# Attention weights of a two-layer trunk: turned by transfers and VectorE instead of TensorE, weighted sums one turn later

## The chip, the core and the metric

The kernel runs on one core of a Trainium2 chip. The metric is the device time of one execution in microseconds (us). Before the change it is 2096.89 us, the median of 3 runs (2096.42 to 2096.99). The engines are TensorE (PE in the profile; PEld is its weight load), VectorE (DVE), ScalarE (ACT), GpSimd (POOL) and SyncE (SP). SP and ACT issue DMA transfers, each into a queue of its own.

## The reference, cut to what matters

Two decoder layers over 256 tokens of width 2048 in float32. Layer 0 is a gated recurrence with an MLP, layer 1 is attention with an MLP. With a block of 256 keys and 256 tokens there are no past blocks, so the attention is plain causal attention with 16 heads of 128:

```python
qkv = (x @ w_qkv).reshape(bsz, seqlen, 3, ATTN_HEADS, ATTN_HEAD_DIM)
q = (_partial_rope(q, cos, sin) * (ATTN_HEAD_DIM ** -0.5)).transpose(0, 2, 1, 3)
k = _partial_rope(k, cos, sin).transpose(0, 2, 1, 3)
...
s_own = jnp.where(k_pos[None, :] <= q_pos[:, None], s_own, NEG_INF)
...
p = jax.nn.softmax(s, axis=-1).astype(v.dtype)
...
        + jnp.einsum("bhcp,bhpd->bhcd", p_own, v_own))
...
return o @ w_out
x = _layer_norm(DEEPNORM_ALPHA * x + y, ln_g[layer, 0], ln_b[layer, 0])
x = _layer_norm(DEEPNORM_ALPHA * x + _sqrelu_mlp(x, mlp_w1[layer], mlp_w2[layer]), ...)
```

## The kernel before, in words

**Turns and blocks.** Every product with a weight matrix is cut into turns. A turn makes 512 output columns out of all 2048 inputs; its weights come in 8 blocks of 256 x 512 numbers (512 KB each). A block is loaded by SP into one of four staging slots `wst`, rounded by ACT into `wh` (line 757), and what the rounding left out is put into `wl` by DVE (line 1014). `wh` and `wl` have eight slots. TensorE multiplies high by high, low by high and high by low part (`turn`, lines 396 to 420; `token_turn` and `token_step`, lines 422 to 440), and the sums stand in PSUM: `banks(0)` and `banks(1)` are its two halves of four banks, and successive turns alternate between them.

**Who waits for whom.** `off` counts blocks from the first of a turn; 0 to 7 are the turn's own and 8 onward are the next turn's. SP may load block X when `wl` of block X-4 is made (line 247). ACT splits a block when it has landed and TensorE is done with block `off` - 7 (lines 754 to 756); DVE follows. During a turn ACT and DVE therefore make the blocks of the next one: `splits(b, START, LATE)` are `off` 9 to 13, then comes the work at the end of the turn, then `splits(b, LATE, NEXT)`, `off` 14 to 16. Each engine works through its list in the written order.

**Attention.** Four groups g of four heads, three turns each: queries, keys, values (lines 693 to 743 on TensorE, 975 to 1003 on ACT, 1405 to 1456 on DVE). In the middle of the values turn TensorE computes the scores of the group (lines 713 and 714). DVE adds the mask and takes the maxima, ACT takes the exponentials (line 989), DVE multiplies by the inverse sums (lines 1445 and 1447) and gives `p_ready`. After the values turn ACT copies the values out of PSUM (line 994, `v_stored`). TensorE turns the weights `prob`, three 128 x 128 pieces a head (line 732); ACT copies each head back out of PSUM (line 997); TensorE makes the weighted sums of the values with them (lines 739 and 741), in float32, into banks 2 and 3 of the half. ACT and DVE split the result into `hid` (lines 1000 and 1453), the input of the output projection, and the next group's queries turn follows. The keys turn of a group waits for that `hid` (line 705), since it uses the same PSUM half.

**Output projection** (`out_unit`, lines 644, 924 and 1302): four turns. Blocks 0 to 5 of a turn use the heads of groups 0 to 2, blocks 6 and 7 those of group 3. `prepare` (line 1181) scales the residual for it. On ACT it begins with a square root (line 926), whose table has to be loaded.

**A pattern that exists already.** In the MLP the squared activations are turned by transfers and VectorE: SP writes four pieces to a buffer in memory and reads it back (lines 312 to 320), DVE transposes 32 x 32 squares (line 1320). There, too, the first two turns of the second product are interleaved (`W2_ORDER`, line 83: blocks 0 to 5 of turn 0, 0 to 5 of turn 1, 6 and 7 of turn 0, 6 and 7 of turn 1; lines 654 to 665).

Of the kernel before, what the change touches and what calls it, by code (L numbers as in the profile page):

```python
# [81 lines left out]
HELD = BLOCKS - KCH  # L82
W2_ORDER = [(t, kb) for lo, hi in ((0, HELD), (HELD, BLOCKS)) for t in range(2) for kb in range(lo, hi)]
# [6 lines left out]
def build_trunk(nc, x, ln_g, ln_b, mlp_w1, mlp_w2, rg_w_in, rg_conv_w, rg_conv_b, rg_gate_a_w,  # L90
                rg_gate_a_b, rg_gate_x_w, rg_gate_x_b, rg_lambda, rg_w_out, moba_w_qkv, moba_w_out,
                rope, out):
    with ExitStack() as ctx:
# [3 lines left out]
        def sem(name):  # L97
            return ctx.enter_context(nc.semaphore(name))
# [39 lines left out]
        prob = f2[:, 0:1536].rearrange("p (h n) -> p h n", n=3 * P)  # L138
        probt = f2[:, 1536:3072].rearrange("p (h n) -> p h n", n=3 * P)
# [70 lines left out]
        pt_done = sem("pt_done")  # L210
        pt_copied = sem("pt_copied")
# [13 lines left out]
        to_quad = by_quad.rearrange("(q t) (i n) -> i t q n", q=GROUP, i=GROUP)  # L225

# [15 lines left out]
        def _(sp):  # L242
# [109 lines left out]
            with sp.Fori(0, NG) as g:  # L352
                for part in range(3):
                    load_turn(moba_w_qkv[0], part * D + g * COLS,
                              B_QKV + (3 * g + part) * BLOCKS)
# [36 lines left out]
        def _(pe):  # L392
# [250 lines left out]

            def out_unit(b, ready, free, n):
                token_pair(hid, b, ready, free)
                last_pair(b + 2 * BLOCKS, ready, free + 2, n)

            def mlp(b0, ready_x, ready_h, free, n):
# [5 lines left out]
                def w2_pair(s):  # L654
                    b = b0 + NG * BLOCKS + s * SLAB_BLOCKS
                    for n, (t, kb) in enumerate(W2_ORDER):
                        if kb == 0:
                            pe.wait_ge(psum_free, free + NG + s * (2 * NG) + t - 1)
                        pe.wait_ge(pair_ready, ready_h + s * (2 * NG) + (kb + 1))
                        pe.wait_ge(wl_done, b + n + 1)  # L660
                        for c in range(kb * KCH, (kb + 1) * KCH):
                            for part, low in ((0, 0), (1, 0), (0, 1)):
                                for a in range(HALVES):
                                    mm = token_step(hid, t, a, c, part, low, n)
                        mm.then_inc(mm_done, 1)
# [27 lines left out]
            for it in range(NG // 2):  # L693
                for j in range(2):
                    g = it * 2 + j
                    X, Y = banks(j), banks(1 - j)
                    b = B_QKV + it * (6 * BLOCKS) + j * (3 * BLOCKS)


                    if g == 0:  # L700
                        begun_turn(1, b, R_LN1)
                    else:
                        turn(xin, j, b, R_LN1)

                    pe.wait_ge(pair_ready, it * 4 + (2 * j + R_ATT))
                    turn(xin, 1 - j, b + BLOCKS, R_LN1)

                    pe.wait_ge(qk_ready, it * 4 + 2 * j + 1)
                    for kb in range(BLOCKS):
                        if kb == BLOCKS // 2:  # L710
                            pe.wait_ge(qk_ready, it * 4 + 2 * j + 2)
                            for h in range(GROUP):
                                pe.matmul(Y[:, h, 0:P], qg[:, h, 0:P], kg[:, h, 0:P], start=True, stop=True)
                                mm = pe.matmul(Y[:, h, P:3 * P], qg[:, h, P:T], kg[:, h, :],  # L714
                                               start=True, stop=True)
                            mm.then_inc(scores_done, 1)
# [773 lines left out]
```

## Time and profile before

| | |
|---|---|
| median of 3 runs | 2096.89 us |
| profiled execution: its own time | 2096.86 us |
| profiled execution: span from the first to the last instruction | 2095.0 us |
| busy: PE, PEld | 100%, 84% |
| busy: DVE, ACT, POOL | 62%, 47%, 1% |
| attention turns in the span (about) | 1005 to 1298 us |
| granted TensorE clock | 1.000 |

The span is what the trace shows; 1.9 us of the execution's own time lie around it. A timeline line has the start of its first instruction, the time from there to the end of the last, and how many instructions were merged (x). Matmuls overlap: one of 512 columns shows 0.39 us, and the next starts 0.23 us after it. A float32 matmul appears as two instructions.

### The profile page before, as it was taken

The page shows a single profiled execution, that of the slowest core. Times are in us where ns is not written, and L with a number is a line of the kernel's source. Part 1 is how long each engine was busy: PE and PEld are TensorE (multiplying, and loading weights), DVE is VectorE, ACT ScalarE, POOL GpSimd, SP SyncE. Part 2 cuts the span into 40 slices and gives each one's busy share as a digit, 9 for nine tenths or more (in the row PEclk, how much of TensorE's full clock was granted, in tenths as well). Part 3 has the DMA queues.
Part 4 walks back from the last instruction along what each step waited for, and adds up shares of the span by engine and source line. Part 5 has one row for each costly group of instructions (what it writes and reads, how often), then busy time and mean ns, then how long its engine had stood idle before and what let it go on. Part 6 is the DMA issues. An engine that isn't in the chain of part 4 may idle for free.

```text
span 2095.0 us, 28820 instructions
## 1 busy us (share of the span) xinstructions
PE 2085.9 (100%) x9918; PEld 1749.5 (84%) x9918; DVE 1290.4 (62%) x1246; ACT 975.1 (47%) x1172; POOL 21.3 (1%) x16
## 2 busy tenths in 40 slices
PE   9999999999999999999999999999999999999999
PEld 8898888888888888888988888888888888888887
DVE  6869666665555565555766667675665554555565
ACT  5596455434444443443644445454434443443442
POOL 0000010000000000000000000010000000000000
PEclk9999999999999999999999999999999999999999
DMA  7665758766766766775654556658666766766763
GB/s 257 195 197 189 235 180 261 250 200 203 236 222 183 238 230 201 219 233 171 193 186 158 168 167 225 202 189 267 216 210 212 241 206 195 243 218 228 241 212 120
DMA packets 233547, 439.80 MB, mean 210 GB/s; under 512 B 15056, under 2 KB 37840, under 8 KB 232432
## 3 DMA queue, kind: packets, MB, share of 16 engines
q1 hardware_dynamic: 232032, 432.79, 65.2%
q10 hardware_dynamic: 1424, 5.77, 0.7%
q8 instruction: 60, 0.98, 0.2%
q14 instruction: 31, 0.25, 0.0%
HBM read 419.63 MB, written 18.87 MB: 209 GB/s over the span
## 4 chain that ended last, share of the span: by engine, by line
PE 99%; DMA 0%; ACT 0%; issue 0%; DVE 0%; ACTq 0%
PE ps L427 75%; PE ps L419 11%; PE ps L416 5%; PE ps L726 1%; PE ps L725 1%; PE ps L724 1%; PE ps L558 1%; PE ps L739 0%; DMA wst<-in_rg_w_in_dram 0%; PE ps L524 0%; PE ps L523 0%; PE ps L525 0%; PE ps L596 0%; PE ps L714 0%; PE ps L599 0%; PE ps L575 0%
## 5 line engine op out<-in xcount | busy, mean ns | idle before, releaser
L1014 DVE TENSOR_TENSOR wl<-wst,wh 128x1024 fp32r<-128x1024 f32 x743 | 887.8, 1219 | 327.3 <-ACT wh L757 324.0
L757 ACT ACTIVATE wh<-wst 128x1024 fp32r<-128x1024 f32 x743 | 769.8, 1059 | 649.1 <-PE ps L427 411.8
L427 PE MATMUL ps<-wh,hid 128*128 128x512 f32 x2560 | 695.9, 390 | 0.0
L427 PEld LDWEIGHTS ps<-wh,hid 128*128 128x128 f32 x2560 | 479.5, 188 | 98.9
L427 PE MATMUL ps<-wh,xin 128*128 128x512 f32 x2048 | 548.9, 389 | 0.0
L427 PEld LDWEIGHTS ps<-wh,xin 128*128 128x128 f32 x2048 | 383.9, 188 | 79.4
L427 PE MATMUL ps<-wl,hid 128*128 128x512 f32 x1280 | 404.6, 389 | 0.0
L419 PE MATMUL ps<-xin,wh 128*128 128x512 f32 x960 | 331.2, 395 | 0.8 <-DVE wl L1014 0.8
L427 PE MATMUL ps<-wl,xin 128*128 128x512 f32 x1024 | 315.2, 389 | 0.0
L427 PEld LDWEIGHTS ps<-wl,hid 128*128 128x128 f32 x1280 | 240.2, 188 | 50.0
L416 PE MATMUL ps<-xin,wl 128*128 128x256 f32 x960 | 256.8, 278 | 0.0
L427 PEld LDWEIGHTS ps<-wl,xin 128*128 128x128 f32 x1024 | 192.2, 188 | 39.9
L419 PEld LDWEIGHTS ps<-xin,wh 128*128 128x128 f32 x960 | 175.9, 188 | 37.8 <-issue 1.3
L416 PEld LDWEIGHTS ps<-xin,wl 128*128 128x128 f32 x960 | 180.4, 188 | 5.3
L1320 DVE STREAM_TRANSPOSE f<-f 128x1024 f32<-128x1024 f32 x32 | 39.9, 1245 | 180.9 <-DMA f<-sq_by_quad 180.9
L934 ACT ACTIVATE hid<-f 128x1024 fp32r<-128x1024 f32 x32 | 34.0, 1063 | 207.4 <-DVE f L1320 207.4
L1204 DVE TENSOR_TENSOR f<-f,ps 128x1024 f32<-128x1024 f32 x36 | 43.9, 1220 | 94.5 <-PE ps L427 94.5
L1344 DVE TENSOR_TENSOR f<-f 128x1024 f32<-128x1024 f32 x32 | 39.2, 1225 | 76.6 <-ACT f L949 76.6
L949 ACT ACTIVATE f<-ps 128x512 f32<-128x512 f32 x64 | 34.7, 595 | 81.0 <-PE ps L427 81.0
L724 PE MATMUL ps<-wh,xin 128*128 128x512 f32 x128 | 50.6, 395 | 0.0
L726 PE MATMUL ps<-wl,xin 128*128 128x512 f32 x128 | 49.8, 389 | 0.0
L725 PE MATMUL ps<-wh,xin 128*128 128x512 f32 x128 | 49.8, 389 | 0.0
(138 smaller groups left out, 835.9 us busy)
## 6 DMA issues: line engine op xcount, KB each, us to landing
wst<-in_mlp_w_dram SPq DMA_DIRECT2D x512, 512.0 KB, 4.7
wst<-in_moba_w_qkv_dram SPq DMA_DIRECT2D x96, 512.0 KB, 4.6
wst<-in_rg_w_in_dram SPq DMA_DIRECT2D x62, 512.0 KB, 4.1
wst<-in_rg_w_out_dram SPq DMA_DIRECT2D x32, 512.0 KB, 4.9
sq_by_quad<-f SPq DMA_DIRECT2D x128, 128.0 KB, 2.5
f<-sq_by_quad SPq DMA_DIRECT2D x32, 512.0 KB, 5.1
wst<-in_moba_w_out_dram SPq DMA_DIRECT2D x32, 512.0 KB, 5.3
f<-in_x_dram SPq DMA_DIRECT2D x8, 256.0 KB, 6.3
```

The lines of the kernel that those rows point to most:

```text
L416: mm = pe.matmul(dst[:, n, 0:T], wl[:, s, w], src[:, c, 0, :], start=False, stop=(c == NC - 1))
L419: pe.matmul(dst[:, n, :], wh[:, s, w], src[:, c, :, :], start=(c == 0), stop=False)
L427: return pe.matmul(banks(half)[:, a, :], src[:, c, part, a * P:(a + 1) * P], (wl if low else wh)[:, s, w], start=(c == 0 and part + low == 0),
L724: pe.matmul(X[:, a, :], xin[:, c, 0, tok], wh[:, s, w], start=(c == 0), stop=False)
L725: pe.matmul(X[:, a, :], xin[:, c, 1, tok], wh[:, s, w], start=False, stop=False)
L726: mm = pe.matmul(X[:, a, :], xin[:, c, 0, tok], wl[:, s, w], start=False, stop=(c == NC - 1))
L757: act.activation(wh[:, off % SPLITS, :], wst[:, slot, :], ACT.Copy).then_inc(wh_done, 1)
L949: act.activation(by_part, by_col, ACT.Relu).then_inc(sq_relu, 1)
L1014: dve.tensor_tensor(wl[:, off % SPLITS, :], wst[:, off % STAGE, :], wh[:, off % SPLITS, :], ALU.subtract).then_inc(wl_done, 1)
L1204: dve.tensor_tensor(res[:, :, cols], res[:, :, cols], banks(half)[:, 0:HALVES, :], ALU.add)\
L1320: dve.transpose(sq_t.rearrange("p c (a i t) -> p i (c a) t", a=HALVES, t=32), quad.rearrange("p i (b r) -> p i b r", r=32)).then_inc(sq_tu ...
L1344: dve.tensor_tensor(sqr, sqr, sqr, ALU.mult).then_inc(psum_free, 1)
```

## The change

1. The products by the inverse sums are written as three instructions of 128 x 512 into another place, `prob_out`, in an order by 32-column parts. Sixteen transfers from SBUF to SBUF, each of 32 partitions x 384 numbers (48 KB), move the parts between quarters of the partitions into `prob_quad` (the place of `prob`): eight issued by SP, ahead of its load of block 7 of the next turn, and eight by ACT, after its copy of the values. DVE then transposes all 32 x 32 squares with one instruction of 128 x 1536 (`turn_p`), after its split of block 9 in the next queries turn.
2. TensorE no longer transposes, and ACT no longer copies turned weights out of PSUM. The weighted sums (`weighted`) are made in the next group's queries turn ahead of its block 5 (`PV_AT`); the split of their result follows `off` 13 of that turn on ACT and DVE.
3. For the last group that place is in the output projection, whose first two turns (n == 2) are interleaved by `W2_ORDER` on all engines; `held_pair` is the loop of the MLP's `w2_pair` made a function.
4. The loops over groups are written out on SP, ACT and DVE. The values turn issues its matmuls in the order of `token_turn` (both token halves for each part) instead of all parts of one half first.

```diff
+MOVES = 16 * GROUP * GROUP
+PV_AT = 5
...
+        prob_out = f2[:, 1536:3072].rearrange("p (q n) -> p q n", q=GROUP)
+        prob_quad = f2[:, 0:1536].rearrange("p (i n) -> p i n", i=GROUP)
...
+        def part_moves(dst, src, of):
+            return [(dst[q * 32:(q + 1) * 32, i, :], src[i * 32:(i + 1) * 32, q, :])
+                    for i in of for q in range(GROUP)]
...
-            with sp.Fori(0, NG) as g:
+            def move_p(g):
+                sp.wait_ge(p_ready, g + 1)
+                for dst, src in part_moves(prob_quad, prob_out, (0, 1)):
+                    sp.dma_start(dst, src).then_inc(p_moved, 16)
+            for g in range(NG):
                 for part in range(3):
...
+                    load_turn(moba_w_qkv[0], part * D + g * COLS, B_QKV + (3 * g + part) * BLOCKS,
+                              {BLOCKS - 1: lambda: move_p(g - 1)} if g and part == 0 else {})
             load_rows(1)
-            with sp.Fori(0, NG) as t:
+            for n, (t, kb) in enumerate(W2_ORDER):
+                if n == BLOCKS - 1:
+                    move_p(NG - 1)
+                load_block(cols_of(moba_w_out[0], t * COLS)[kb], n, B_MO + n)
+            with sp.Fori(2, NG) as t:
...
+            def weighted(g):
+                pe.wait_ge(pt_ready, g + 1)
+                pe.wait_ge(v_stored, g + 1)
+                for h in range(GROUP):
+                    o_ap = banks(g % 2)[:, 2 + h // 2, (h % 2) * T:(h % 2 + 1) * T]
+                    pe.matmul(o_ap, vg[:, 0, h * P:(h + 1) * P], probt[:, h, 0:2 * P], start=True, stop=False)
+                    mm = pe.matmul(o_ap[:, P:T], vg[:, 1, h * P:(h + 1) * P], probt[:, h, 2 * P:3 * P],
+                                   start=False, stop=True)
+                mm.then_inc(pv_done, 1)
...
             def out_unit(b, ready, free, n):
-                token_pair(hid, b, ready, free)
+                if n == 2:
+                    held_pair(hid, b, ready, free, {0: lambda: pe.wait_ge(bias_ready, NG),
+                                                     PV_AT: lambda: weighted(NG - 1)})
+                else:
+                    token_pair(hid, b, ready, free)
...
+                else:
+                    pe.wait_ge(bias_ready, g)
+                    turn(xin, j, b, R_LN1, {PV_AT: lambda: weighted(g - 1)})
...
-                    pe.wait_ge(p_ready, g + 1)
-                    for h in range(GROUP):
-                        for k in range(3):
-                            mm = pe.transpose(Y[:, h, k * P:(k + 1) * P], prob[:, h, k * P:(k + 1) * P],
-                                              ident[:, :])
-                        mm.then_inc(pt_done, 1)
...
+                splits(b0, b0 // BLOCKS, START, LATE)
+                if n == 2:
+                    weighted_hi(NG - 1)
+                splits(b0, b0 // BLOCKS, LATE, NEXT)
...
+            def move_p(g):
+                act.wait_ge(p_ready, g + 1)
+                for dst, src in part_moves(prob_quad, prob_out, (2, 3)):
+                    act.dma_start(dst, src).then_inc(p_moved, 16)
...
+                act.activation(vg, banks(j)[:, 0:2, :], ACT.Copy).then_inc(v_stored, 1)
+                move_p(g)
+                splits(bv, nv, LATE, NEXT)
...
+            def turn_p(g):
+                dve.wait_ge(p_moved, MOVES * (g + 1))
+                dve.transpose(f2[:, 1536:3072].rearrange("p (b i t) -> p i b t", i=GROUP, t=32),
+                              prob_quad.rearrange("p i (b r) -> p i b r", r=32)).then_inc(pt_ready, 1)
...
+                    if n == 2 and t == 0:
+                        splits(b, START, START + 1)
+                        turn_p(NG - 1)
+                        prepare(n - 1, t)
+                        splits(b, START + 1, LATE)
+                        weighted_lo(NG - 1)
...
+                        if g and part == 0:
+                            splits(b, START, START + 1)
+                            turn_p(g - 1)
+                            splits(b, START + 1, LATE)
+                            weighted_lo(g - 1)
...
+                    for k in range(3):
+                        a = min(k, 1)
+                        ins = dve.tensor_tensor(by_part[:, k],
+                                                prob[:, :, k * P:(k + 1) * P].rearrange("p h (q r) -> p h q r", r=32),
+                                                stat[:, :, 6 + a:7 + a].unsqueeze(2)
+                                                .to_broadcast([P, GROUP, GROUP, 32]), ALU.mult)
+                    ins.then_inc(p_ready, 1)
```

## Rows read from the trace of the kernel before

**Rows 1.** The page: busy time of the engines, share of the span, instructions.
```profile
PE 2085.9 (100%) x9918; PEld 1749.5 (84%) x9918; DVE 1290.4 (62%) x1246; ACT 975.1 (47%) x1172; POOL 21.3 (1%) x16
```

**Rows 2.** What TensorE waited for, whole span: us in total, times, longest us.
```profile
PE ps L739 <- ACT f L997: 1.1, 4, 0.3
```

**Rows 3.** Timeline, end of group 0's values turn: start, us, engine, line, [idle before <-releaser].
```profile
1073.39 0.40 PE L726 MATMUL ps<-wl,xin 128*128 128x512 f32 x1
...
1073.62 1.48 PE L732 MATMUL ps<-ident,f 128*128 128x128 f32 x12
...
1075.37 0.67 PE L739 MATMUL ps<-f 128*128 128x256 f32 x2 [0.28 <-ACT f L997]
...
1077.98 0.71 PE L419 MATMUL ps<-xin,wh 128*128 128x512 f32 x2
```

**Rows 4.** The line of the transposes: count, ns min/median/max, first and last start.
```profile
L732 PE MATMUL ps<-ident,f x48: 270/272/275, 1073.6 to 1294.6; 128*128 128x128 f32 x48
```

**Rows 5.** Timeline of TensorE around group 0's scores, in the values turn.
```profile
1060.11 0.38 PE L713 MATMUL ps<-f 128*128 128x128 f32 x2
...
1062.95 0.40 PE L725 MATMUL ps<-wh,xin 128*128 128x512 f32 x1
```

**Rows 6.** Where group 1's values turn begins; from the chain, first turns of output projection.
```profile
1122.47 0.40 PE L724 MATMUL ps<-wh,xin 128*128 128x512 f32 x1
...
1297.99 81.62 PE ps L427 x360
```

**Rows 7.** Timeline of DVE, from the end of group 0's softmax on.
```profile
1070.67 0.69 DVE L1445 TENSOR_TENSOR f<-f,stat 128x512 f32<-128x512 f32 x1
...
1072.41 3.49 DVE L1014 TENSOR_TENSOR wl<-wst,wh 128x1024 fp32r<-128x1024 f32 x3
...
1084.92 1.23 DVE L1014 TENSOR_TENSOR wl<-wst,wh 128x1024 fp32r<-128x1024 f32 x1 [0.61 <-ACT wh L757]
```

**Rows 8.** Timeline of ACT, the same stretch.
```profile
1073.82 1.03 ACT L994 ACTIVATE f<-ps 128x1024 f32<-128x1024 f32 x1 [0.58 <-PE ps L726]
...
1079.30 2.95 ACT L757 ACTIVATE wh<-wst 128x1024 fp32r<-128x1024 f32 x3
1083.83 1.06 ACT L757 ACTIVATE wh<-wst 128x1024 fp32r<-128x1024 f32 x1 [1.58 <-PE ps L416]
```

**Rows 9.** Timeline of ACT, start of the output projection.
```profile
1302.01 1.28 ACT L926 ACT_TABLE_LOAD   x1
```

**Rows 10.** Three weight loads in a row, windows from 1073.7 and 1293.4 us: starts, us to landing.
```profile
L248 SPq DMA_DIRECT2D wst<-in_moba_w_qkv_dram x3: 372/372/372, 1073.8 to 1076.1; - x3
...
DMA to landing us min/median/max: 3.6/4.4/4.7
...
L248 SPq DMA_DIRECT2D wst<-in_moba_w_out_dram x3: 373/373/373, 1293.5 to 1295.8; - x3
...
DMA to landing us min/median/max: 3.7/5.7/5.9
```

**Rows 11.** The MLP's transfers: SP's timeline; the last row is two loads' time to landing.
```profile
354.68 0.34 SPq L320 DMA_DIRECT2D f<-sq_by_quad  x1
355.28 1.02 SPq L248 DMA_DIRECT2D wst<-in_mlp_w_dram  x2
...
DMA to landing us min/median/max: 5.7/6.0/6.4
```

**Rows 12.** SP's issues, four and then a load; and the line's counts.
```profile
372.06 1.83 SPq L316 DMA_DIRECT2D sq_by_quad<-f  x4
374.14 0.40 SPq L248 DMA_DIRECT2D wst<-in_mlp_w_dram  x1
...
L316 SPq DMA_DIRECT2D sq_by_quad<-f x128: 332/431/857, 329.9 to 2001.8; - x128
```

**Rows 13.** Landing of the MLP's 128 KB pieces; VectorE's transposes.
```profile
DMA to landing us min/median/max: 2.0/2.5/4.3
...
L1320 DVE STREAM_TRANSPOSE f<-f 128x1024 f32<-128x1024 f32 x32 | 39.9, 1245 | 180.9 <-DMA f<-sq_by_quad 180.9
```

More of the change, by code:

```diff
@@ L209, in build_trunk @@
         v_stored = sem("v_stored")
[L210 to L211 removed]
+        p_moved = sem("p_moved")
+        pt_ready = sem("pt_ready")
         pv_done = sem("pv_done")
@@ L654, in w2_pair @@
                 def w2_pair(s):
[L655 to L665, printed above, removed]
+                    held_pair(hid, b0 + NG * BLOCKS + s * SLAB_BLOCKS, ready_h + s * (2 * NG),
+                              free + NG + s * (2 * NG))
                 def w2(s):
@@ new lines, in _ @@
+            for g in range(NG):
+                j = g % 2
+                X, Y = banks(j), banks(1 - j)
+                b = B_QKV + 3 * g * BLOCKS
+                if g == 0:
+                    begun_turn(1, b, R_LN1)
+                else:
+                    pe.wait_ge(bias_ready, g)
+                    turn(xin, j, b, R_LN1, {PV_AT: lambda: weighted(g - 1)})
+                pe.wait_ge(pair_ready, R_ATT + 2 * g)
+                turn(xin, 1 - j, b + BLOCKS, R_LN1)
+                pe.wait_ge(qk_ready, 2 * g + 1)
+                for kb in range(BLOCKS):
+                    if kb == BLOCKS // 2:
+                        pe.wait_ge(qk_ready, 2 * g + 2)
+                        for h in range(GROUP):
+                            pe.matmul(Y[:, h, 0:P], qg[:, h, 0:P], kg[:, h, 0:P], start=True, stop=True)
+                            mm = pe.matmul(Y[:, h, P:3 * P], qg[:, h, P:T], kg[:, h, :], start=True, stop=True)
+                        mm.then_inc(scores_done, 1)
+                    pe.wait_ge(wl_done, b + 2 * BLOCKS + kb + 1)
+                    for c in range(kb * KCH, (kb + 1) * KCH):
+                        for part, low in ((0, 0), (1, 0), (0, 1)):
+                            for a in range(HALVES):
+                                mm = token_step(xin, j, a, c, part, low)
+                    mm.then_inc(mm_done, 1)
@@ L926, in out_unit @@
                 act.activation(tok[:, 1, 0:1], eps[:, 0:1], ACT.Sqrt)
-                for j in range(2):
-                    splits(b0 + j * BLOCKS, b0 // BLOCKS + j, START, NEXT)
+                splits(b0, b0 // BLOCKS, START, LATE)
+                if n == 2:
+                    weighted_hi(NG - 1)
+                splits(b0, b0 // BLOCKS, LATE, NEXT)
+                splits(b0 + BLOCKS, b0 // BLOCKS + 1, START, NEXT)
                 last_pair(b0 + 2 * BLOCKS, b0 // BLOCKS + 2, n)
@@ L1404, in _ @@
             dve.wait_ge(consts, 6)
-            with dve.Fori(0, NG // 2) as it:
-                for j in range(2):
-                    g = it * 2 + j
-                    b = B_QKV + it * (6 * BLOCKS) + j * (3 * BLOCKS)
+            for g in range(NG):
+                    j = g % 2
+                    b = B_QKV + 3 * g * BLOCKS
                     for part, dst in enumerate((qg, kg)):
-                        splits(b + part * BLOCKS, START, LATE)
-                        links = it * 12 + 6 * j + 3 * part
-                        n = it * 4 + 2 * j + part
+                        if g and part == 0:
+                            splits(b, START, START + 1)
+                            turn_p(g - 1)
+                            splits(b, START + 1, LATE)
+                            weighted_lo(g - 1)
+                        else:
+                            splits(b + part * BLOCKS, START, LATE)
+                        links = 6 * g + 3 * part
+                        n = 2 * g + part
                         add_hh((j, 1 - j)[part], dst, hl_copied, T_RO + n + 1).then_inc(qk_link, 1)
```

140 lines of the change are left out of this document (58 added, 82 removed).

## Prediction, made before the changed kernel was built or run

> **What bounds the kernel now.** I read the page's busy times first: TensorE is busy for 2085.9 of the 2095.0 us of the span, VectorE for 62% and ScalarE for 47% [rows 1]. The end is set by TensorE's instruction stream, so a microsecond counts only where TensorE issues less or stands still. The list of what TensorE waited for comes next: in the attention only the first weighted sum after ScalarE's copies, 1.1 us in four waits [rows 2]. Then the timeline at the seam between a values turn and the next queries turn: last matmul of the values at 1073.39, twelve transposes from 1073.62, first weighted sum at 1075.37 after 0.28 us of idleness, first matmul of the next turn at 1077.98 [rows 3]. The seam stands four times; the transposes number 48, from 1073.6 to 1294.6 us [rows 4]. All else of attention is already hidden, so the change can gain at the seams and can lose only where TensorE gets a new wait.
>
> **What it takes off TensorE.** The transposes and the idleness behind them reach from 1073.62 to 1075.37 [rows 3]: 1.75 us a group. The weighted sums stay: they take 1075.37 to 1077.98, 2.61 us, and will stand between two blocks of a turn instead of between two turns. The price of such an insertion is seen at the scores, the same eight float32 products in the middle of a turn: from 1060.11 to the second ordinary matmul at 1062.95 is 2.84, less one ordinary matmul of 0.23 makes 2.61 [rows 5]. So moving them costs nothing. Sum on TensorE: 4 x 1.75 = **7.0 us less**. Against the profiled execution's own time of 2096.86 us (span 2095.0 and 1.9 around it, and 0.03 under the median) that is **2089.9 us if nothing new waits**. The values turn's new order has the same matmuls; the order it takes is that of the output projection's, where 360 matmuls take 81.62 us [rows 6], 0.227 each, as in the values turn (1073.39 to 1073.62 [rows 3]): nothing. The written-out loops: I take nothing, since TensorE's attention code was written out before and shows no other wait.
>
> **What the weights must now go through, and when TensorE asks.** I put the end of group 0's values turn at 1073.62. A queries turn of 8 blocks: two turns last from 1077.98 [rows 3] to 1122.47 [rows 6], so a block is 44.49 / 16 = 2.78 us, and block 5 is asked for at 1073.62 + 5 x 2.78 = **1087.5**. In the output projection a block is 81.62 / 30 = 2.72 [rows 6]; the last group's transposes end their starts at 1294.6, eleven of 0.12 after the first [rows 3, 4], so its values turn ends at about 1293.4, and item 5 is asked for at 1293.4 + 13.6 = **1307.0**.
>
> Now the chain to `pt_ready`:
>
> *VectorE's products.* Before, they occupy 1070.67 to 1072.41 [rows 7]. Three of 128 x 512, each 0.69 and overlapping by 0.08, take 1.8 to 1.9: `p_ready` at 1072.6. The strided output has no row; bounds 0 to +0.5 (one more 0.69 less the overlap), I take 0.
>
> *SP.* It waits for `p_ready` ahead of its load of block 7. Behind it in its queue stand the loads of blocks 7, 8 and 9. The first of those left at 1073.8 before [rows 10], when `wl` of block 3 was made, so the wait itself delays nothing; the eight issues do. Four issues in a row take 1.83 and the next load starts 2.08 after the first [rows 12], 0.46 for each further one, so eight delay the load by 2.08 + 4 x 0.46 = 3.9: it leaves at 1076.6 instead of 1073.8. One issue is between 0.33 and 0.86 [rows 12]; I keep these ends for the range and take 0.46, the spacing of a burst whose pieces are nearest in kind. Blocks 8 and 9 then follow at once, 0.6 us apart.
>
> *When block 9 lands.* Before, the three loads were issued at 1073.8 to 1076.1, the last landed 4.7 after its issue, 7.0 after the first issue [rows 10]. In the MLP three 512 KB transfers issued 0.6 apart had the third landed at 355.9 + 6.4 = 362.3, 7.6 after the first [rows 11]; so issuing them closer together lands them no sooner. I take 7.2: block 9 is there at **1083.8** (bounds 7.0 and 7.6). For the projection's weights the same three took 1295.8 + 5.9 - 1293.5 = 8.2 [rows 10]; there the first leaves at 1293.4 + 3.0 = 1296.4, and block 9 lands at 1304.6.
>
> *ScalarE.* Its copy of the values ends at 1074.85 [rows 8]. The eight issues at 0.46 end at 1078.5. Three splits behind them took 2.95 before, from 1079.30 to 1082.25 [rows 8]; now they would begin 0.8 us earlier, so the copies out of PSUM that went away (1.63 us) and the wait for the sums pay for the issues. But the splits of blocks 7 and 8 now wait for their loads, and that of block 9 for its own: it starts at 1083.8. Before, it began at 1083.83 [rows 8], so this costs ScalarE little by itself.
>
> *VectorE.* Its split starts 1.09 after ScalarE's (1083.83 to 1084.92 [rows 7, 8]) and gives way 1.14 later. `turn_p` sits behind it, since it was put after block 9 in VectorE's list. Its 128 x 1024 relative takes 1.245 [rows 13]; 1536 columns make 1.87. So it ends at 1083.8 + 1.09 + 1.14 + 1.87 = 1087.9, with 0.1 for TensorE to take notice: 1088.0, **0.5 us late, in each of three groups**. The moved pieces aren't what it waits for: the last leaves ScalarE by 1078.5 and pieces of 128 KB land in 2.0 to 4.3 us [rows 13], by 1082.8.
>
> *The last group.* ScalarE's block 8 lands some 1.3 us ahead of block 9 (6.4 against 5.7 plus 0.6 between issues [rows 11]), at 1303.3; its split of 1.05, the table load of 1.28 [rows 9] and the root bring the start of block 9's split to about 1305.8, and `pt_ready` to 1305.8 + 4.1 = 1309.9 by that path; if the loads land as soon as in the other groups, 1.0 sooner, 1308.9. I take 1309.6: **2.6 us late**, between 1.0 and 4.0.
>
> *Behind these waits.* What stands behind `turn_p` on VectorE are the splits of blocks 10 to 13. TensorE has eight slots made ahead, so they are wanted more than 10 us later. The keys turn waits for the low part of the sums: they are made at 1087.5 + 0.5 + 2.6 = 1090.6, block 5 ends at 1093.4, ScalarE's split 13 and its high part (1.06 and 1.03 [rows 8]) end at 1095.5, VectorE's low part (as long as a split, 1.23 [rows 7]) at 1096.8; the keys turn begins at 1073.62 + 22.2 + 2.6 + 0.5 = 1098.9. Two microseconds of cover: no wait. In the projection the last heads are wanted at item 12, 15 us after the sums: none.
>
> **Sum.** 2096.86 - 7.0 + 3 x 0.5 + 2.6 = **2094.0 us** (-0.14%), by the median the same.
>
> **A rule against the change.** TensorE pays 0.12 us for each transpose here (1.48 for twelve [rows 3]), and the cost is real only because TensorE is the engine that never rests [rows 1]. The Trainium skill, "VectorE: DVE Perf Modes", section "Rules for kernel authors", says to use TensorE for a 128 x 128 transpose if a PSUM destination will do. As a rule for one operation the trace agrees with it: VectorE's single instruction alone is longer than the twelve transposes. It has no term for which engine bounds: by it the transposes should stay, 2096.9 us, where the rows allow down to 2089.9.
>
> **The rivals.**
> - *All of it is hidden.* If a move's issue costs near the lowest row, 0.33, or block 9 lands 0.5 sooner, the three groups lose nothing, and the last one 0 to 2.8: 2089.9 to 2092.6 us. For it: ScalarE's own list, were the loads there, would reach block 9's split by 1081.5. Against: no burst of three loads landed under 7.0 us [rows 10, 11]. Chance 0.36.
> - *The issues are dear, and it ends slower.* The place is SP's queue ahead of block 7. Each 0.1 us on an issue puts 0.8 us on four waits, 3.2 us in all. From 0.68 us an issue instead of 0.46 the waits reach 11.2 us and the change turns over 0.2% slower. At the longest row, 0.86 [rows 12], it is 2094.0 + 12.8 = 2106.8 us. For it: ScalarE and SP issue at the same time for 2 us, and no row shows moves between partitions. Against: the typical issue is 0.43. Chance 0.07.
> - *The moves land one after another.* Eight in a queue, each 2.0 us at the least [rows 13], would have ScalarE's last land at 1074.9 + 16 = 1090.9, the transpose end 2 us later at 1092.9, 5.4 us late; in four groups 21.6, so 2111.5 us. Against: the MLP's four pieces are issued within 1.83 us and one lands in 2.5 [rows 12, 13], so they overlap. Chance 0.04. Beside it, the Trainium skill, "DMA: Bandwidth & Descriptors", section "Bandwidth", has transfers under 64 KB ruled by their descriptors and asks for large ones; these are 48 KB.
> - *It doesn't free TensorE at the seam,* for instance since the queries turn then waits there for its own blocks or for PSUM: about 2096.9 us. Nothing in the list of waits hints at it. Chance 0.03.
> - *The forecast,* waits of 2.7 to 8.9 us in sum: 2092.6 to 2098.8 us. Chance 0.50.
>
> **How the numbers follow.** A measurement of this kernel can tell about 0.2% from no change, 4.2 us: faster is under 2092.7, slower over 2101.1. Faster: 0.36 and 0.02 of the forecast's lower edge, 0.38. Slower: 0.11. Same: 0.51. The range takes in the hidden case and the forecast with its upper bound: 2089.6 to 2099.0; the two slower rivals and a little are left out.
>
> **What the profile after should show.** No transposes at the seam, and the values turn's last matmul followed by the next turn's first after 0.23 us: right if the four seams shrink to nothing. TensorE's waits should name the first weighted sum, released by VectorE's transpose, four times, the last the longest. ScalarE should wait for the landing of blocks 7 to 9, whose loads leave about 2.8 us later than before. SP's eight issues should take about 3.6 us. If TensorE has no such wait, the landing or issue term was too large; if it has but the transpose itself waited for the moves, the term of the moves was too small. A TensorE wait in the keys turn, or a longer insertion than 2.6 us, would make the sum wrong in its other parts.

## The result, and the profile after

The changed kernel takes **2101.49 us** (median of 13 runs, 2098.10 to 2104.47) where the kernel before takes 2096.89 us beside it (2096.42 to 2097.84): ratio 1.0021, 95% interval 1.0013 to 1.0029. It is slower by 4.6 us. The forecast was 2094.0 us with a range up to 2099.0; the time lies outside it, and on the side to which 0.11 had been given. Its runs also lie 6.4 us apart, those before 1.4.

The profiled execution of the changed kernel took 2101.49 us, its span is 2099.4 us (before: 2096.86 and 2095.0). The page's busy times:

```profile
PE 2084.0 (99%) x9870; PEld 1746.9 (83%) x9870; DVE 1297.6 (62%) x1254; ACT 968.2 (46%) x1155; POOL 21.3 (1%) x16
```

TensorE has 48 instructions fewer than in [rows 1], but the span is longer: it stands still. What TensorE waited for in the whole span (total, times, longest, in us) answers to [rows 2]:

```profile
PE ps L668 <- DVE f L1328: 8.6, 4, 3.9
PE ps L508 <- POOL ident L392: 2.0, 1, 2.0
```

Line 668 is the first weighted sum, line 1328 VectorE's new transpose. The seam of [rows 3] is gone: the last matmul of the values and the first of the next queries turn follow each other at the ordinary pace (TensorE's timeline; the second line starts at 1073.28, the ordinary 0.23 us behind the last of the two in the first line). The wait stands where the sums now are:

```profile
1072.83 0.62 PE L445 MATMUL ps<-wl,xin 128*128 128x512 f32 x2
1073.28 0.61 PE L437 MATMUL ps<-xin,wh 128*128 128x512 f32 x2
...
1087.04 0.27 PE L434 MATMUL ps<-xin,wl 128*128 128x256 f32 x1
1088.83 0.70 PE L668 MATMUL ps<-f 128*128 128x256 f32 x2 [1.51 <-DVE f L1328]
```

From the start of the last ordinary matmul to the first sum is 1.79 us where 0.11 is usual: group 0 loses 1.68 us, groups 1 and 2 lose 1.67 and 1.87, the last 4.04. The chain that set the end, in order of time, runs for group 0 from VectorE's products through SP to that sum (start, us, what):

```profile
1071.54 0.70 DVE f L1509
1072.26 0.62 SPq L364
...
1077.00 0.62 SPq L364
...
1077.67 0.58 SPq L257
...
1078.30 0.48 SPq L257
...
1078.82 5.92 DMA wst<-in_moba_w_qkv_dram
1084.76 1.07 ACT wh L774
1085.89 1.11 issue
1087.00 1.78 DVE f L1328
...
1088.83 0.70 PE ps L668 x2
```

Line 364 is SP's issue of the moves, line 257 that of the weight loads. This is, link by link, the chain of the forecast; what differs is the first link. SP's eight issues last 5.37 us instead of 3.6 (the timeline, then SP's line of moves and the time from issue to landing):

```profile
1072.26 5.37 SPq L364 DMA_DIRECT2D f<-f  x8
1077.67 3.76 SPq L257 DMA_DIRECT2D wst<-in_moba_w_qkv_dram  x4
...
L364 SPq DMA_DIRECT2D f<-f x32: 512/604/841, 1072.3 to 1297.5; - x32
...
DMA to landing us min/median/max: 1.8/1.9/2.3
```

In the last group the chain has one link more, as the forecast had said: ScalarE's table load stands ahead of its split of block 9 (the first of the three in the second line).

```profile
1306.02 1.28 ACT L943 ACT_TABLE_LOAD   x1
...
1307.42 2.95 ACT L774 ACTIVATE wh<-wst 128x1024 fp32r<-128x1024 f32 x3
```

The last group has something more, which the forecast did not have at all. TensorE's timeline there:

```profile
1311.46 1.22 PE L668 MATMUL ps<-f 128*128 128x256 f32 x2 [3.88 <-DVE f L1328]
1312.48 0.63 PE L669 MATMUL ps<-f 128*128 128x128 f32 x2
...
1315.14 0.60 PE L668 MATMUL ps<-f 128*128 128x256 f32 x2
1315.58 0.38 PE L669 MATMUL ps<-f 128*128 128x128 f32 x2
```

After 4 us of idleness the same pair of products takes 1.22 us where it took 0.70 in group 0, and is back to 0.60 only at the fourth head. A view of stretches (each engine's busy time, then the granted clock, 1.00 being 2.4 GHz) shows why: the share is 0.61 here, a mixture of 2.4 and 1.2 GHz, and 1.00 on both sides.

```profile
1293.80:1307.40 13.60, 13.60 (x61) 11.08 (x59) 6.06 (x6) 5.58 (x6) 0.00 (x0) 1.00 0.77 220
1311.40:1315.80 4.40, 4.33 (x17) 3.79 (x17) 4.37 (x5) 1.06 (x1) 0.00 (x0) 0.61 0.33 111
1315.80:1325.00 9.20, 9.20 (x43) 7.61 (x42) 4.97 (x5) 3.79 (x4) 0.00 (x0) 1.00 0.69 228
```

The eight sums take 4.25 us instead of 2.63: 1.6 us lost to the clock.

The clock did not fall like this in every run. A fall of this length takes the mean clock of a run to 0.999. Five of the thirteen have a mean of 1.000 and took 2098.1 to 2100.57 us, the other eight 2100.82 to 2104.47; the median of the first is 2099.2, of the others 2102.5. So part of the spread goes with the clock, and without a fall the changed kernel is still about 2 us slower than the one before.

**The account.** Gained at four seams, 6.9 us. Lost: waits of 1.68 + 1.67 + 1.87 + 4.04 = 9.3 us; the slow clock, 1.6; queries and keys turns of groups 2 and 3 that run 0.4 us longer a group for a reason not found (below), 0.8. The attention began 0.3 us earlier in this execution. Sum: -6.9 + 9.3 + 1.6 + 0.8 - 0.3 = +4.5 us, for a span that is 4.4 longer.

### The profile page after: what moved, and what is told of

It is laid out like the page before. It is cut to its first block, busy times and chain, and to the rows that moved or that the text cites. A ratio compares the mean times of both kernels' runs of the same rounds, so it can differ in the third digit from the quotient of the medians.

```text
span 2099.4 us, 28201 instructions
## 1 busy us (share of the span) xinstructions
PE 2084.0 (99%) x9870; PEld 1746.9 (83%) x9870; DVE 1297.6 (62%) x1254; ACT 968.2 (46%) x1155; POOL 21.3 (1%) x16
## 4 chain that ended last, share of the span: by engine, by line
PE 95%; DMA 1%; SPq 1%; DVE 1%; ACT 1%; issue 1%; ACTq 0%
PE ps L445 77%; PE ps L437 9%; PE ps L434 5%; SPq L364 1%; DMA wst<-in_moba_w_qkv_dram 1%; PE ps L576 1%; PE ps L668 0%; ACT f L1020 0%; PE ps L541 0%; PE ps L542 0%; PE ps L543 0%; PE ps L614 0%; DVE f L1328 0%; PE ps L753 0%; DMA wst<-in_moba_w_out_dram 0%
## 5 line engine op out<-in xcount | busy, mean ns | idle before, releaser
L445 PE MATMUL ps<-wh,xin 128*128 128x512 f32 x2304 | 618.1, 390 | 0.0
L445 PEld LDWEIGHTS ps<-wh,xin 128*128 128x128 f32 x2304 | 431.8, 188 | 89.1
L445 PE MATMUL ps<-wl,xin 128*128 128x512 f32 x1152 | 354.6, 389 | 0.0
L445 PEld LDWEIGHTS ps<-wl,xin 128*128 128x128 f32 x1152 | 216.2, 188 | 44.9
L1382 DVE TENSOR_TENSOR hid<-f,hid 128x1024 fp32r<-128x1024 f32 x32 | 39.2, 1226 | 3.0
L898 ACT ACTIVATE f<-ps,prm 128x128 f32<-128x128 f32 x96 | 36.1, 478 | 4.3 <-PE ps L576 4.3
L405 POOL TENSOR_SCALAR f<-f,mv,tok 128x512 f32<-128x512 f32 x6 | 19.5, 3263 | 1365.4 <-DVE tok L1258 1365.4
```

The costliest lines, as they stand in the source:

```text
L445: return pe.matmul(banks(half)[:, a, :], src[:, c, part, a * P:(a + 1) * P], (wl if low else wh)[:, s, w], start=(c == 0 and part + low == 0),
L898: ins = act.activation(norm_t[:, c, h * P:(h + 1) * P], ps[:, bank, q * P:(q + 1) * P], ACT.Identity, scale=prm[:, gain:gain + 1], bias=pr ...
L1382: dve.tensor_tensor(hid[:, rows, 1, :], sq_t, hid[:, rows, 0, :], ALU.subtract)\
```

## Experiments

Theory A: SP's issues of moves cost 0.6 us each, push the loads of blocks 7 to 9 back, and through ScalarE's and VectorE's lists the transpose; the long wait of the last group also lets the clock fall. Against it stood: the moves themselves land too late (C); the trouble is in TensorE's own insertion or goes on to the keys turn (B); the clock falls anyway (D); the written-out code costs something (E). They ran on three chips (the first four, the next four, the last three), on each of which the kernel before was run beside them; it took 2098.47, 2098.35 and 2098.37 us there, 1.5 us more than beside the result above. Each version is set against the one of its own chip, so a gain of some 8 us here is not all the change's. The first four expectations count from 2096.9 us; what they promised is best read as a distance from the kernel before.

**The sums one block later.**
```diff
-PV_AT = 5
+PV_AT = 6
```


> The changed kernel with the weighted sums one block later (ahead of block 6 instead of 5). Theory A (SP's eight issues, 0.6 us each and not 0.46, push the loads of blocks 7 to 9 back, these push VectorE's transpose past block 5, and the long wait of the last group lets TensorE's clock fall): a block more is 2.8 us of cover, so the waits of 1.7 us in three groups go, the last falls from 3.9 to about 1.2 us, the clock stays, and nothing else waits: 2096.9 - 7.0 + 1.2 + some 0.5 = 2091.6 us. Rival B (the loss is in what TensorE does around the sums, or a later place only moves the wait to the keys turn, which needs the low part of the sums): a wait appears in the keys turn and the time stays above 2096 us.

Measured: 2090.45 us (2090.21 to 2091.93), before 2098.47; ratio 0.9964, interval 0.9950 to 0.9977, so 8.0 us faster. TensorE's waits:

```profile
PE ps L668 <- DVE f L1328: 0.4, 1, 0.4
PE ps L437 <- DVE wl L1060: 0.3, 1, 0.3
```

One constant turns a loss (4.6 us above, 2.7 when it was run again, below) into a gain. B falls: no wait on the sums' low part shows; the 0.3 us are on a weight block near the start. The last group's wait was 0.4, less than the 1.2 expected, and the gain 8.0 us, more than the 5.3 expected. What a seam is worth without a wait can be read where the scores of groups 0 and 1 begin, in this kernel and then in the one before (its group 0 is in [rows 5], at 1060.11):

```profile
1059.84 0.38 PE L752 MATMUL ps<-f 128*128 128x128 f32 x2
...
1131.26 0.38 PE L752 MATMUL ps<-f 128*128 128x128 f32 x2
```
```profile
1133.36 0.38 PE L713 MATMUL ps<-f 128*128 128x128 f32 x2
```

They are 71.42 us apart instead of 73.25: 1.83 us a group, 7.3 in all. Less the wait of 0.4 this is 6.9 us; most of the rest of the 8.0 is that the kernel before is slower on this chip. Here, too, the insertion can be read without a wait ahead of it:

```profile
1089.88 0.27 PE L434 MATMUL ps<-xin,wl 128*128 128x256 f32 x1
1090.00 0.59 PE L668 MATMUL ps<-f 128*128 128x256 f32 x2
...
1092.53 0.47 PE L437 MATMUL ps<-xin,wh 128*128 128x512 f32 x1
1092.85 0.28 PE L434 MATMUL ps<-xin,wl 128*128 128x256 f32 x1
```

2.53 us to the next ordinary matmul and 0.09 more after it (0.32 to the next where 0.23 is usual): 2.6 in all, as the scores' rows had said [rows 5].

**SP's moves behind its three loads.**
```diff
-                              {BLOCKS - 1: lambda: move_p(g - 1)} if g and part == 0 else {})
+                              {2: lambda: move_p(g - 1)} if g and part == 1 else {})
...
-                if n == BLOCKS - 1:
+                if n == BLOCKS + 2:
                     move_p(NG - 1)
```


> The changed kernel with SP's eight moves behind its loads of blocks 7, 8 and 9 instead of ahead of block 7; the place of the sums as in the changed kernel. Theory A (the loads pushed back by the moves are the cause): the three loads leave when they did before the change, block 9 lands at about 7 us after block 7's issue, VectorE's transpose ends some 86.6 - 73.3 = 13.3 us after the values turn and TensorE asks at 13.9: no wait in three groups, 0 to 0.5 us in the last, 2090 to 2091 us. Rival C (the moves themselves are what is late: their issue and their landing): they now land later still, behind three loads, so VectorE waits for them and TensorE's waits stay at 1.7 us or grow: 2098 us or more.

Measured: 2092.97 us (2091.12 to 2094.73), before 2098.47; ratio 0.9974, interval 0.9962 to 0.9985, 5.5 us faster where 6 to 7 were expected. The waits on the sums sank from 8.6 to 1.4 us in two places:

```profile
PE ps L668 <- DVE f L1328: 1.4, 2, 1.3
```

So the loads are the cause, since the moves now come later and TensorE waits less. But C has a part here: issued behind three loads, SP's moves of group 0 land after 4.7 us and not 1.9. ScalarE's moves, in a queue that carries no loads, do no better: 5.2 us (the third line). So it isn't only their place in SP's queue that makes them land late; what both have in common is that the three loads are on their way at the same time. VectorE waits for moves 0.5 us in group 2 and 0.7 in the last (its timeline), and this can account for 0.8 of TensorE's 1.4 us at most.

```profile
L364 SPq DMA_DIRECT2D f<-f x8: 590/608/726, 1076.6 to 1081.4; - x8
...
DMA to landing us min/median/max: 3.8/4.7/5.7
...
DMA to landing us min/median/max: 3.7/5.2/5.5
...
1301.67 1.78 DVE L1328 STREAM_TRANSPOSE f<-f 128x1536 f32<-128x1536 f32 x1 [0.70 <-DMA f<-f]
```

**Only the last group's sums later.**
```diff
-                                                     PV_AT: lambda: weighted(NG - 1)})
+                                                     PV_AT + 2: lambda: weighted(NG - 1)})
```


> The changed kernel with the last group's weighted sums two items later (ahead of item 7 of the output projection instead of 5); the three other groups untouched. Theory A with its clock part (only the long wait of 3.9 us lets the clock fall, and that makes the runs differ by 6 us): three waits of 1.7 us stay, the last is gone, the clock is 1.000 in every run, the runs lie within 1 us, and the time is 2096.9 - 7.0 + 5.1 + some 0.5 = 2095.5 us. Rival D (the clock falls behind the short waits too): the clock is under 1.000 in some runs, the runs still spread over several us, and the median is above 2097 us.

Measured: 2095.92 us (2095.26 to 2097.96), before 2098.47; ratio 0.9988, interval 0.9979 to 0.9997: 2.6 us faster than before, and 5.1 under the changed kernel as it ran on the next chip (2101.01, below). The changed kernel was not run on this chip, so the 5.1 is rough; the last wait with its clock had cost 4.0 and 1.6, 5.6. The three others stand:

```profile
PE ps L668 <- DVE f L1328: 4.8, 3, 1.7
```

The profiled execution has the full clock throughout, and the runs lie 2.7 us apart instead of 6.4. So behind waits of up to 1.7 us the clock held in this execution. Two of the eleven runs have a mean clock of 0.999, one of them the slowest. That alone proves no fall behind a wait: the traces of several versions show the lower clock in the last 1 to 2 us of the span, when TensorE has finished, and a mean of 0.999 can come from there (the last version below has it so). That the clock never falls behind the short waits isn't shown either way.

**Loops and order alone.** The kernel before with the loops written out and the values turn's matmuls in the new order:
```diff
+                            for part, low in ((0, 0), (1, 0), (0, 1)):
+                                for a in range(HALVES):
+                                    mm = token_step(xin, j, a, c, part, low)
...
-            with dve.Fori(0, NG // 2) as it:
+            for it in range(NG // 2):
```


> The kernel before with only two parts of the change: the loops over groups written out on SP, ACT and DVE, and the values turn's matmuls in the new order. Theory A: neither moves anything, 2096.9 us within 0.5. Rival E (the written-out code or the order has a price of its own, seen as the keys turns of groups 1 and 2 that are 0.4 us longer after the change): 0.8 us or more above the kernel before.

Measured: 2098.29 us (2097.50 to 2099.08) beside 2098.47, ratio 0.9998, interval 0.9989 to 1.0007. These parts cost nothing that can be measured. In its profile the queries and keys turns of groups 2 and 3 took 44.87 us together instead of 44.48, as after the change: the 0.4 us belong neither to the moves nor to the sums. (The expectation names these turns by the sums that stand in them, those of groups 1 and 2.) In the profile of the version with the sums at block 6 they don't appear.

**The changed kernel once more,** on the chip of the next three.

> The changed kernel once more, unchanged, to stand on the same chip as the three beside it. Expected: 4 to 5 us above the kernel before, with runs some 6 us apart.

Measured: 2101.01 us (2099.45 to 2105.17), before 2098.35; ratio 1.0012, interval 1.0003 to 1.0021. The loss is 2.7 us on this chip, less than the 4 to 5 expected: the kernel before is 1.5 us slower here and the changed one is not; why is open. The waits are the same, 8.7 us, the longest 3.8. In this trace the clock fell only when TensorE had been at work again for 1.1 us (from 1312.2, the first sum starting at 1311.08), and the sums took 4.1 us.

**TensorE kept busy in the last wait.**
```diff
             def weighted(g):
+                if g == NG - 1:
+                    keep_warm(16, 6)
                 pe.wait_ge(pt_ready, g + 1)
```


> The changed kernel with 16 small products of constants (128 x 128, float32, 0.22 us each, 3.5 us in all, into a bank that nothing else uses then) issued by TensorE ahead of the last group's wait; no result changes. They lie inside a wait of 3.9 us. Theory A's clock part (it is idleness at the long wait that makes the clock fall, and this costs 1.6 us in the profiled run and up to 6 in others): the last wait shrinks to about 0.4 us, the clock is 1.000, the runs lie within 2 us, and the median is 1.5 to 2.5 us under the changed kernel's. Rival D (the clock falls for another reason, or at the short waits): same median and same spread as the changed kernel.

```profile
1308.48 3.74 PE L508 MATMUL ps<-ones 128*128 128x128 f32 x32
1312.05 0.60 PE L670 MATMUL ps<-f 128*128 128x256 f32 x2
...
1308.40:1312.10 3.70, 3.70 (x35) 3.66 (x34) 3.38 (x3) 2.29 (x3) 0.00 (x0) 1.00 0.84 270
1312.10:1315.00 2.90, 2.90 (x20) 2.65 (x19) 2.87 (x3) 1.06 (x1) 0.00 (x0) 1.00 0.31 108
```

The first line is the filling work, the second the first sum, now 0.60 us; below them the same stretches by window, with the clock at 1.00. The data come as late as ever, but the sums take 2.5 us instead of 4.1: idleness of TensorE was what the clock fell for in this place. The median is 2100.46 us (2099.33 to 2102.55), ratio 1.0011, interval 1.0002 to 1.0020. The spread shrank to 3.2 us, with 2 expected, and the mean clock is 1.000 in nine of eleven runs where it was so in three, but the median gained 0.55 us and not the 1.5 to 2.5 expected; the two profiled executions differ by 0.8 us of span, this one having begun its attention 0.85 us later. Set apart by their mean clock, the runs say more: the medians of those at 1.000 agree, 2099.9 with the filling work (nine runs) and 2099.8 without (three), while that of the eight others of the changed kernel is 2101.1. By these few runs the fall costs 1.3 us where it happens (3.3 in the thirteen runs of the result), and a loss of 1.5 us to the kernel before is there without it.

**The transpose ahead of block 9's split.**
```diff
-                            splits(b, START, START + 1)
                             turn_p(g - 1)
-                            splits(b, START + 1, LATE)
+                            splits(b, START, LATE)
```
The same exchange is made for the last group, in the output projection.


> The changed kernel with VectorE's transpose ahead of its split of block 9 instead of behind it. Theory A (the moved pieces land some 3 us before the transpose; it is late since it queues behind block 9's split, whose load was pushed back): the transpose starts 1.2 us earlier in three groups and over 2 us earlier in the last, where ScalarE's table load no longer lies ahead of it; waits of 0.5 us three times and 1.6 us once, clock 1.000, about 3.5 us under the kernel before. Rival C (the moves' landing is what it waits for): no difference from the changed kernel.

Measured: 2092.86 us (2092.31 to 2094.05), before 2098.35; ratio 0.9975, interval 0.9965 to 0.9984: 5.5 us faster than before, better than the 3.5 expected. The four waits add up to 1.3 us, the longest 0.6. VectorE begins the transpose right behind block 8's split, without any wait for the moves:

```profile
1083.02 2.58 DVE L1038 TENSOR_TENSOR wl<-wst,wh 128x1024 fp32r<-128x1024 f32 x2 [2.20 <-ACT wh L774]
1085.52 1.77 DVE L1328 STREAM_TRANSPOSE f<-f 128x1536 f32<-128x1536 f32 x1
```

C is refuted for the changed kernel: with SP's moves ahead of the loads, the pieces had long landed. The last of ScalarE's is issued at 1077.8 in group 0 and none of its moves there takes over 4.3 us, so all are in place by 1082.1.

**Both remedies,** the moves behind the loads and the sums at block 6.

> Both remedies in one: SP's moves behind the three loads, and the sums ahead of block 6. Theory A: no wait on the weights is left anywhere, so all of the 7.0 us (and the 0.1 us a seam by which the insertion is cheaper than the old seam) is gained: 7 to 8.5 us under the kernel before, and no more than 0.5 us under the version with the sums at block 6 alone. Rival B: a wait in the keys turn takes some of it back.

Measured: 2089.94 us (2089.50 to 2090.72), before 2098.35; ratio 0.9961, interval 0.9948 to 0.9975: 8.4 us faster than before, and no wait of TensorE on the weights left. VectorE waits for moves in three groups, 2.4 us in all, and TensorE doesn't feel it. It beats the kernel before and the changed one; that it beats the one with the sums at block 6 alone (0.5 us, in the medians, and on two chips) isn't certain.

**The sums one block earlier.** `PV_AT = 4`.

> The changed kernel with the sums one block earlier (ahead of block 4). Theory A: each of the four waits grows by the one block of 2.8 us, to about 4.5 us three times and 6.6 us once, 20 us in all; and if it is the length of the idleness that makes the clock fall (not at 1.7 us, but at 3.9), it now falls behind all four, at some 1.5 to 2 us each: 2098.4 - 7.3 + 20 + 6 to 8 = 2117 to 2119 us. Rival F (the fall in the output projection is a matter of that place and not of the idleness): one fall as before, 2113 us or less.

Measured: 2120.20 us (2116.94 to 2122.71), before 2098.37; ratio 1.0099, interval 1.0082 to 1.0116: 21.8 us slower in the medians, a little over the 2117 to 2119 expected. Waits of 19.6 us, as expected; and the first three sums, which had run at full clock in the changed kernel, now run at 0.50 to 0.53:

```profile
PE ps L668 <- DVE f L1328: 19.6, 4, 5.9
...
1089.80:1095.00 5.20, 5.12 (x16) 4.41 (x17) 2.26 (x3) 0.00 (x0) 0.00 (x0) 0.50 0.86 293
1169.30:1174.40 5.10, 5.08 (x16) 4.37 (x17) 2.20 (x2) 0.33 (x1) 0.00 (x0) 0.50 0.96 322
1248.30:1253.20 4.90, 4.80 (x16) 4.15 (x17) 2.28 (x3) 0.28 (x1) 0.00 (x0) 0.53 0.91 313
```

The same products, after 4.4 to 4.7 us of idleness, take 4.8 to 5.1 us instead of 2.63, so 2.2 to 2.5 us more each, where 1.5 to 2 were expected. It is not a matter of the output projection (F falls), and one block of lateness costs more than itself: four blocks of 2.8 us are 11, and the time is 19 us above the changed kernel's.

**What an issue costs.** Two versions, one execution each: shorter runs, and another destination. Neither gives TensorE the right weights; the first leaves out a third of them, the second leaves their quarters unexchanged.
```diff
-            return [(dst[q * 32:(q + 1) * 32, i, :], src[i * 32:(i + 1) * 32, q, :])
+            return [(dst[q * 32:(q + 1) * 32, i, 0:256], src[i * 32:(i + 1) * 32, q, 0:256])
```
```diff
+        aside = nc.dram_tensor("p_aside", (P, 12 * P), F32, kind="Internal").ap()
...
+            return [(aside[q * 32:(q + 1) * 32, i * 384:(i + 1) * 384], src[i * 32:(i + 1) * 32, q, :])
```


> The changed kernel with each of the sixteen transfers moving 256 instead of 384 numbers of a partition (1024 instead of 1536 bytes in a run; a third of the weights isn't moved). What one issue costs: 0.62 us in the changed kernel, 0.43 for the MLP's pieces in runs of 1024 bytes. If the run's length is the reason, the issues fall to 0.43 and TensorE's waits to about 0.3 us, 2 us in the last group; if not, issues stay at 0.6 us and the waits at 1.7 and 3.8.

> The changed kernel with the sixteen transfers, same size and number, going from SBUF to a buffer in memory instead of to other partitions of SBUF (the transposed weights are then not the right ones). If an SBUF address on both sides is what makes an issue cost 0.62 us, they fall to the 0.43 of the MLP's pieces, which also go to memory; if not, they stay at 0.6.

SP's line of moves, first with a third less in each, then with memory as the destination, and there TensorE's wait:

```profile
L364 SPq DMA_DIRECT2D f<-f x32: 512/602/839, 1072.4 to 1296.7; - x32
```
```profile
L366 SPq DMA_DIRECT2D p_aside<-f x32: 327/421/438, 1072.9 to 1292.0; - x32
...
PE ps L670 <- DVE f L1330: 1.9, 1, 1.9
```

The size changes nothing: 602 ns against 604, waits of 7.9 us, and 2100.57 us in all. The destination does: 421 ns on SP (447 on ScalarE), the MLP's 431 of [rows 12], though number, size and shape are those of the change and the two engines issue at the same time as before. With it the three first waits are gone, the last is 1.9 us, and the time is 2094.03 us, 4.3 under the 2098.37 of the kernel before there. That is the forecast's own condition, issues 0.46 us apart, with waits 2.2 us shorter in sum than it had for them (1.9 for 4.1). That the time is the forecast's 2094.0 to the digit is luck: the forecast meant 2.9 us under the kernel before.

## Why the prediction was wrong

**Right: what TensorE gives up.** The forecast took 4 x 1.75 = 7.0 us off; the trace has 6.9, and without waits it is 7.3 (four times 1.83). The versions almost without waits are 8.0 and 8.4 us faster, on chips where the kernel before is 1.5 us slower. The insertion at 2.61 us was right.

**Right: the chain and its order.** The forecast said what would be late (the transpose), by what (SP's issues, then the loads, then ScalarE's and VectorE's splits) and that the moved pieces would not be what it waits for. Each link but SP's issues held: block 9 of group 0 landed 7.1 us after block 7's issue (forecast 7.2), and from there to the sum it was 4.1 us (4.2). The keys turn's cover held. (One slip of a tenth: 1072.6 and 3.9 make 1076.5 for SP's load, not 1076.6.)

**Wrong: the price of an issue.** The step took 0.46 us an issue, "the spacing of a burst whose pieces are nearest in kind", and had SP's load of block 7 leave 3.0 us after the values turn. It left 4.4 us after it in group 0 (1073.28 to 1077.67) and 4.3 in the others, for issues of 0.604 us that started 0.66 to 0.68 apart on average. These 1.3 to 1.4 us appear, within 0.2, in the first three waits: 1.7 to 1.9 for 0.5. The last is 4.0 for 2.6: 1.3 us from the issues, and the rest since the forecast took 1309.6, a little under its path through the table load (1309.9), and the trace took that path. Together 5.2 us. The burst taken as the model goes to memory, and the version that moves to memory shows the destination to be what decides. The row's own longest, 0.86, was kept for a rival only: the likeliest case's range ended at waits of 8.9 us. That rival, "the issues are dear", was the right one in its mechanism, at a chance of 0.07. At 0.66 to 0.68 an issue its rule of 3.2 us per 0.1 gives 2100.4 to 2101.0 us, over the range's end of 2099.0.

**Missing: the clock.** The forecast counted an idle microsecond of TensorE as one microsecond. After 4 us of idleness the granted clock was at its lower level, which cost 1.6 us more in the profiled execution, and the earlier sums (`PV_AT = 4`) show it four times; in five of the thirteen runs of the changed kernel no such fall shows in the mean clock. No row of before has a TensorE wait in the attention over 0.3 us, so its sum could not show this; but a wait of up to 4.0 us was forecast with nothing said of what might follow it. Without this term the time is still outside the range by little or not at all: the five runs took 2098.1 to 2100.57 us, with a median of 2099.2.

**The sum again.** 2094.0 and 5.2 of longer waits, 1.6 of clock, 0.8 of slower turns, less 0.3 for the earlier start: 2101.3; the profiled execution took 2101.49.

**The rules that were weighed.** By the Trainium skill, "VectorE: DVE Perf Modes", section "Rules for kernel authors", a 128 x 128 transpose goes to TensorE if a PSUM destination will do. The changed kernel came out on that side, but not for that reason: taking the transposes off TensorE is worth 7.3 us as soon as nothing waits. The rival with the moves landing one after another is refuted: SP's were issued some 0.65 us apart and landed 1.8 to 2.3 us after their issue, ScalarE's after 2.0 in the median and 5.1 at most. By the Trainium skill, "DMA: Bandwidth & Descriptors", section "Bandwidth", transfers under 64 KB are ruled by their descriptors. The trace agrees as far as it goes: with a third less in each move SP's still landed after 1.9 us in the median.

**What stays open.** Why the clock falls behind the long wait in some runs and not in others. Why one run in eleven or thirteen of the changed kernel has a mean clock of 0.997, which would be some 12 us at half speed and 6 us of time (an estimate from the mean): its traced executions had 3.4 us of slow clock in mid-course only, and those runs have no trace. Why matmuls run 2% slower for about one turn of 22 us in groups 2 and 3 of some executions, in kernels with and without the change. Why the kernel before takes 1.5 us more beside the experiments than beside the result, and the changed kernel doesn't. Why an issue with SBUF on both sides takes 0.18 us more. And whether GpSimd, idle here, could issue the moves, which was not tried.

## What to carry to other kernels

When work is taken off the bounding engine and handed to a longer way round, place the moment at which that engine asks for the result by the slowest link of the way, with a block to spare: here one constant turned 2.7 to 4.6 us of loss into 8.0 of gain. A queue that carries the main stream pays for every small transfer put ahead of it, not in bytes but in issues; count them by a row with the same kind of source and destination. Put behind the loads that are wanted next, they no longer hold these up, but land later themselves, here after 5 us instead of 2, so their reader needs the room. Price a forecast wait of the bounding engine of several microseconds above its length: here a wait of 4.0 us cost up to 1.6 more.

## What the runs showed of the hardware

- An issue of a transfer of 32 partitions x 1536 bytes takes 0.60 us on SP and 0.61 on ACT with SBUF at both ends, 0.42 and 0.45 with memory as the destination; 1024 bytes instead of 1536 make no difference.
- SP's moves ahead of its three loads of 512 KB landed after 1.9 us. With the three loads under way moves took 4.7 us behind the loads in SP's queue, and 5.2 in ACT's queue, which has no loads in it.
- TensorE's granted clock was at 1.2 GHz (0.5) after idleness of 4 to 6 us in the middle of dense work, and the eight sums of 2.63 us then took 4.1 to 5.1. It need not fall: in 5 of 13 and 3 of 11 runs of the kernel with a wait of 4.0 us the mean clock is 1.000. After idleness of 1.9 us and less in the same places the traced executions had 2.4 GHz, and with filling work of 3.7 us in the wait it stayed there.
- The kernel with such a wait varied by 6 us from run to run. Those without one varied by 1.2 to 3.6, the kernel before by 1.4 to 2.3.
